# Router logits in four column groups, and token rows stored without their norm factor

## The chip, the cores and the metric

One NeuronCore of a Trainium2 chip runs the whole program. The metric is device time in microseconds (us) of one execution, lower is better. A run's time is a little longer than its span, which is the time from the first to the last instruction in the profile.

## The reference, cut to what matters

The program is one inference step of a two-layer encoder with D_MODEL = 1024, for 256 prompt frames and 64 sample frames (320 token rows, here called T). Layer 0 is a pooling mixer and a dense SwiGLU, then comes a shared K/V projection, and layer 1 is windowed attention followed by a top-2-of-8 mixture of experts. The change is in the mixture:

```
h = _rmsnorm(x, g_ffn)                     # x * rsqrt(mean(x*x) + eps) * g, per token row
logits = h @ w_router + b_router           # 1024 -> 8, in fp32
vals, idx = top_k(logits, 2); gates = softmax(vals)
y = sum over e of gate[:, e] * ((silu(h @ w1[e]) * (h @ w3[e])) @ w2[e])
```

A token goes to two experts only, so the kernel gathers the rows of each expert's tokens. The norm factor r of a token is a scalar per row: h = r * (x * g).

## The kernel before, in words

All activations are kept transposed (128 features x 320 tokens per chunk, eight chunks, KC = 8). Each fp32 weight unit of 1 MB (128 x 2048) is loaded into `raw` by SyncE's queue (6 slots), split by ScalarE (`hi`, L426: high part, two halves) and VectorE (`lo`, L1199: what is left, two halves) into a ring of 3, and multiplied by TensorE as three fp32r products (`mm3`, all matmuls at L720). The order of the work on each engine is written out by hand, and semaphores join the engines.

The stretch around the change lies between the attention's output projection and the first expert:

1. Output projection: four units, `dense` two column chunks each (f = 0, 1). VectorE adds each chunk into `xT` (L1466), ScalarE squares it (L438) and writes x * g to `hT` (L454, `weighted`, counted by `h_ready`), VectorE sums the squares (L1224).
2. TensorE: `rows(0)` transposes chunks 0 to 3 of `hT` back to token rows (L1037, 12 transposes into three PSUM banks); `logits` multiplies `hT` blocks of 128 or 64 tokens (as weights) by the 8 router columns (24 matmuls, each two instructions); `norm_columns` gives the sums of squares per token row; `rows(1)` transposes chunks 4 to 7.
3. ScalarE: root of the sums (L447, L448), the table load for Exp (L433), then six copies of the transposed rows to `hrow` (L655), each with the norm factor `rsc` as its scale, so that they wait for `rs_ready`; the gates' Exp (L659) stands among them.
4. SyncE's queue stores the rows to `rows_dram` in three transfers (L297), one per block of token rows, each when both halves of its block are copied.
5. VectorE: logits * rsc + bias (L1480), top two (L1484, L1487), selection `sel` (L1499). TensorE counts positions (`pos_done`); VectorE makes the one-hot matrices `Pm` (L1539), then the softmax gates (L1543 to L1548); TensorE multiplies `Pm` by the slot numbers; VectorE derives the gather index `ix` (L1550, L1552) after the gates. GpSimd splits the gates into three bf16 parts (`gpart`, L392 to L398) in four steps that start at `gate_ready`, and only then comes to its waits for `rows_stored` and `ix_ready` and to the indirect gather (L389).
6. TensorE fills its time with the embedding product of layer 1 (`embed`, eight chunks of six matmuls, whose banks are copied out by ScalarE at L530).
7. When the gathered rows land, TensorE transposes them (L1075), ScalarE and VectorE split them (L665, L1204), and the first expert starts.

The experts run in a loop: 8 turns here, 42 units each. In a turn ScalarE applies Silu to the gate product (L685, 7 times), VectorE multiplies by the up product (L1584), and the row results are scaled by the gate of their slot, `gs` (L707). SyncE's queue starts the loads of the loop once the first gather has landed.

Of the kernel before, what the change touches and what calls it, by code (L numbers as in the profile page):

```python
# [18 lines left out]
BF16 = mybir.dt.bfloat16  # L19
# [6 lines left out]
P = 128  # L26
# [40 lines left out]
EBANK = (4, 0, 5, 2, 6, 3, 4, 0)  # L67
LBANK = (7, 1, 7)
# [8 lines left out]
def build(nc, A):  # L77
    ctx = ExitStack()
    with ctx:
# [27 lines left out]
        wr = sb("wr", [P, KC, NE])  # L107
# [16 lines left out]
        tg = sb("tg", [P, 3, 5], BF16)  # L124
# [4 lines left out]
        sn, gs = sb("sn", [P, 2]), sb("gs", [P, 1])  # L129
# [35 lines left out]
        def squared(k):  # L165
# [49 lines left out]
        pT_done, pT_ready, pv_done, oh_ready, ol_ready = sem("pT_done"), sem("pT_ready"), sem("pv_done"), sem("oh_ready"), sem("ol_ready")  # L215
        lg_done, top_ready, gexp_ready, sel_ready, pos_done, routed = (sem(n) for n in (
            "lg_done", "top_ready", "gexp_ready", "sel_ready", "pos_done", "routed"))
        hrow_done, hrow_ready = sem("hrow_done"), sem("hrow_ready")
# [15 lines left out]
        def _(sp):  # L234
# [93 lines left out]
        def _(pool):  # L328
# [61 lines left out]

            pool.wait_ge(gate_ready, 1)
# [7 lines left out]
            pool.wait_ge(rows_stored, 48)  # L399
# [14 lines left out]
        def _(act):  # L414
# [236 lines left out]
            for n in range(6):  # L651
                t, half = n // 2, n % 2
                r = TS if t == 2 else P
                act.wait_ge(hrow_done, 4 + t if half else t + 1)
                nc.scalar.activation(hrow[0:r, t, 512 * half:512 * half + 512], PS[0:r, EBANK[n], :], ACT.Copy,  # L655
                                     scale=rsc[0:r, t:t + 1]).then_inc(hrow_ready, 1)
                if n == 3:
                    act.wait_ge(top_ready, 1)
                    nc.scalar.activation(rt[:, :, 1], rt[:, :, 0], ACT.Exp).then_inc(gexp_ready, 1)  # L659
# [15 lines left out]
            def turn(at, last):  # L675
# [5 lines left out]
                for n in range(NU):  # L681
                    kind, b = SEQ[n // 2]
                    if n % 2 and kind == "g":
                        act.wait_ge(unit_done, at(NU) + (Q_MOE + n + 1))
                        nc.scalar.activation(sgm[:, b % 2, :], PS[:, 2 + 2 * (b % 2), :], ACT.Silu).then_inc(msilu_done, 1)  # L685
# [7 lines left out]
                    if n == NU - 1:  # L693

                        act.wait_ge(gs_ready, at(1) + 1)
# [22 lines left out]
        def _(pe):  # L718
# [150 lines left out]
            def embed(layer, q, ns):  # L869
# [4 lines left out]
                for n in ns:  # L874
                    c = ORDS[layer][n]
                    bank = EBANK[n] if layer else c
                    if not layer:
                        pe.wait_ge(x_ready, KC + n + 1)
                    elif n < 6:
# [153 lines left out]
            def rows(half):  # L1033
                for t in range(3):
                    r = TS if t == 2 else P
                    for q in range(4):
                        last = nc.tensor.transpose(PS[0:r, EBANK[2 * t + half], P * q:P * q + P], hT[:, 4 * half + q, P * t:P * t + r], ident[:, :])  # L1037
                    last.then_inc(hrow_done, 1)

            def logits(k0, k1, blocks):  # L1040
                for k in range(k0, k1):
                    for t in blocks:
                        r = TS if t == 2 else P
                        last = mm(PS[0:r, LBANK[t], 8 + NE * t:8 + NE * t + NE], hT[:, k, P * t:P * t + r], wr[:, k, :], k == 0, k == KC - 1,
                                  skip_group_check=True)
                return last
# [7 lines left out]
            pe.wait_ge(h_ready, 4)  # L1054
            rows(0)
            pe.wait_ge(small_loaded, 48)
            pe.wait_ge(h_ready, 6)
            logits(0, 6, (0, 1))
            pe.wait_ge(h_ready, KC)
            logits(6, KC, (0, 1))  # L1060
            norm_columns(4)
            logits(0, KC, (2,)).then_inc(lg_done, 1)
            rows(1)
# [14 lines left out]
            def slot_info():  # L1078
                for t in range(3):
                    last = mm(PS[:, 1, 0:5], Pm[:, t, :], tg[:, t, :], t == 0, t == 2)  # L1080
                last.then_inc(slots_done, 1)

            embed(1, Q_EMB, range(1))
# [4 lines left out]
            embed(1, Q_EMB, range(1, 4))  # L1088
            pe.wait_ge(P_ready, 1)
            slot_info()  # L1090
            embed(1, Q_EMB, range(4, KC))
# [93 lines left out]
        def _(v):  # L1185
# [99 lines left out]
            norm(1)  # L1285
            v.wait_ge(pool_stored, 32)
# [191 lines left out]
            for t in range(3):  # L1478
                r = TS if t == 2 else P
                last = nc.vector.scalar_tensor_tensor(out=lg[0:r, t, :], in0=PS[0:r, LBANK[t], 8 + NE * t:8 + NE * t + NE], scalar=rsc[0:r, t:t + 1],  # L1480
# [39 lines left out]
            def take_slots(count):  # L1520
                v.wait_ge(slots_done, count)
                nc.vector.reduce_sum(sn[:, 0:1], PS[:, 1, 0:2], AX.X)
                nc.vector.reduce_sum(sn[:, 1:2], PS[:, 1, 2:5], AX.X).then_inc(sn_ready, 1)
# [10 lines left out]
            def use_gates(count):  # L1534
                nc.vector.tensor_copy(gs[:, :], sn[:, 1:2]).then_inc(gs_ready, 1)
# [4 lines left out]
            last.then_inc(number_ready, 1)  # L1540
            v.wait_ge(gexp_ready, 1)
# [7 lines left out]
            v.wait_ge(number_done, 1)  # L1549
            nc.vector.reduce_sum(sn[:, 0:1], PS[:, 1, 0:2], AX.X).then_inc(number_taken, 1)  # L1550
            v.wait_ge(number_taken, 1)
            nc.vector.tensor_scalar(ix[:, :], sn[:, 0:1], float(T), float(T - 1), ALU.add, ALU.min).then_inc(ix_ready, 1)  # L1552
# [9 lines left out]
            nc.vector.reduce_sum(sn[:, 1:2], PS[:, 1, 2:5], AX.X).then_inc(sn_ready, 1)  # L1562
# [165 lines left out]
```

## Time and profile before

| what | us |
|---|---|
| median of 3 runs | 1494.49 (1494.62, 1494.49, 1489.64) |
| the profiled execution's own time | 1490.69 |
| its span | 1488.9 |
| last output-projection matmul issued | 466.02 |
| last chunk of `hT` written | 467.89 |
| first expert matmul issued | 489.44 |
| one expert turn | about 118.7 |

The mean granted TensorE clock is 0.995 of full speed. Times in the rows are us from the start of the span. In a timeline a row is: start, duration, engine, line, operation, output <- inputs, partitions x elements, count; in brackets, the idle time before it and what ended it. Consecutive like instructions are merged into one row with a count (x12). PEld rows are weight loads that run beside the matmuls. An fp32 matmul (both operands fp32) appears as two instructions.

### The profile page before, as it was taken

What the parts mean: (1) busy time and instruction counts of PE and PEld (TensorE: products, weight loads), DVE (VectorE), ACT (ScalarE), POOL (GpSimd) and SP (SyncE); (2) the same over time, 40 slices, a digit from 0 to 9 for tenths busy, and PEclk for the clock granted to TensorE, in tenths of its full rate; (3) what the DMA queues carried; (4) which work ended last, traced back from release to release, by engine and by line L of the source; (5) the groups of instructions that cost most, each with busy time, mean ns of one, the idle gap of its engine ahead of it and who ended that gap; (6) DMA issues with size and microseconds to landing.
All of it is one profiled execution on the core that took longest, in us unless ns stands there. A gap on an engine that the chain in (4) does not pass through costs nothing.

```text
span 1488.9 us, 23197 instructions
## 1 busy us (share of the span) xinstructions
PE 1458.2 (98%) x8006; PEld 1283.3 (86%) x8006; DVE 1201.0 (81%) x1438; ACT 1015.3 (68%) x1291; POOL 34.9 (2%) x62
## 2 busy tenths in 40 slices
PE   6999999999999999999999999999999999999997
PEld 6999999999979788888888888888888888888787
DVE  6744545458775899999999999899999999999897
ACT  5433333356685777877877877787777787787776
POOL 2000000000000000000000000000000000000000
PEclk9999999999998999999999999999999999999999
DMA  9444434435502899999999999999999999999951
GB/s 351 174 142 166 144 142 147 164 123 191 191 30 93 320 380 391 364 398 389 359 394 383 357 403 380 371 390 375 379 388 375 387 371 383 390 359 401 377 199 36
DMA packets 65459, 437.59 MB, mean 294 GB/s; under 512 B 8595, under 2 KB 10259, under 8 KB 14336
## 3 DMA queue, kind: packets, MB, share of 16 engines
q1 hardware_dynamic: 62224, 426.77, 74.1%
q0 software_dynamic: 2768, 9.89, 2.6%
q8 instruction: 31, 0.51, 0.1%
q10 hardware_dynamic: 416, 0.26, 0.1%
q14 instruction: 20, 0.16, 0.0%
HBM read 428.12 MB, written 8.77 MB: 293 GB/s over the span
## 4 chain that ended last, share of the span: by engine, by line
PE 91%; DVE 5%; ACT 2%; DMA 1%; issue 1%; SPq 0%; DVEq 0%; POOLq 0%; ACTq 0%
PE PS L720 88%; PE PS L1116 2%; DVE s_Sl L1199 1%; DMA s_raw<-in_w_trunk 1%; DVE s_Al L1212 0%; PE PS L1075 0%; ACT s_Sh L426 0%; DMA s_G<-rows_dram,s_ix 0%; DVE s_xT L1278 0%; DVE s_st L1425 0%; DVE s_G L1367 0%; ACT s_hT L438 0%; DVE s_Al L1204 0%; DVE s_G L1440 0%; PE PS L1149 0%
## 5 line engine op out<-in xcount | busy, mean ns | idle before, releaser
L1199 DVE TENSOR_TENSOR s_Sl<-s_raw,s_Sh 128x1024 fp32r<-128x1024 f32 x798 | 938.9, 1220 | 130.1 <-ACT s_Sh L426 126.9
L426 ACT ACTIVATE s_Sh<-s_raw 128x1024 fp32r<-128x1024 f32 x798 | 799.8, 1052 | 220.1 <-PE PS L720 219.4
L720 PE MATMUL PS<-s_Sh,s_Ah 128*128 128x512 f32 x1344 | 529.5, 394 | 1.2 <-DVE s_Al L1204 1.2
L720 PE MATMUL PS<-s_Sh,s_Al 128*128 128x512 f32 x1344 | 523.8, 390 | 0.0
L720 PE MATMUL PS<-s_Sl,s_Ah 128*128 128x512 f32 x1344 | 523.2, 389 | 0.0
L720 PE MATMUL PS<-s_Ah,s_Sh 128*128 128x320 f32 x1008 | 314.2, 312 | 5.8 <-DVE s_Al L1212 2.4
L720 PE MATMUL PS<-s_Al,s_Sh 128*128 128x320 f32 x1008 | 311.8, 309 | 0.0
L720 PE MATMUL PS<-s_Ah,s_Sl 128*128 128x320 f32 x1008 | 311.8, 309 | 0.0
L720 PEld LDWEIGHTS PS<-s_Sh,s_Al 128*128 128x128 f32 x1344 | 252.3, 188 | 53.1
L720 PEld LDWEIGHTS PS<-s_Sh,s_Ah 128*128 128x128 f32 x1344 | 252.3, 188 | 52.1 <-issue 1.4
L720 PEld LDWEIGHTS PS<-s_Sl,s_Ah 128*128 128x128 f32 x1344 | 252.6, 188 | 50.6
L720 PEld LDWEIGHTS PS<-s_Ah,s_Sh 128*128 128x128 f32 x1008 | 189.5, 188 | 8.2 <-DVE s_Sl L1199 3.4
L720 PEld LDWEIGHTS PS<-s_Al,s_Sh 128*128 128x128 f32 x1008 | 189.7, 188 | 0.2
L720 PEld LDWEIGHTS PS<-s_Ah,s_Sl 128*128 128x128 f32 x1008 | 189.5, 188 | 0.0
L486 ACT ACTIVATE s_sq<-s_sq 128x640 f32<-128x640 f32 x14 | 10.3, 739 | 74.9 <-DVE s_sq L1300 63.5
L1204 DVE TENSOR_TENSOR s_Al<-PS,s_Ah 128x512 fp32r<-128x512 f32 (+1 forms) x88 | 55.2, 647 | 6.7 <-ACT s_Ah L665 2.7
L685 ACT ACTIVATE s_G<-PS 128x512 f32<-128x512 f32 x56 | 33.6, 599 | 36.9 <-PE PS L720 36.9
L490 ACT ACTIVATE s_Ah<-s_G 128x640 fp32r (+1 forms) x14 | 10.2, 738 | 51.3 <-PE PS L720 47.0
L1204 DVE TENSOR_TENSOR s_Al<-s_G,s_Ah 128x640 fp32r<-128x640 f32 x14 | 11.5, 825 | 41.6 <-ACT s_Ah L490 41.6
L1300 DVE TENSOR_TENSOR s_sq<-PS,s_rstd 128x640 f32<-128x640 f32 x14 | 11.5, 824 | 40.8 <-PE PS L720 40.8
L1584 DVE TENSOR_TENSOR s_G<-s_G,PS 128x512 f32<-128x512 f32 x56 | 38.1, 680 | 0.0
L1116 PEld LDWEIGHTS PS<-s_ident,s_G 128*128 128x128 f32 x224 | 27.8, 141 | 7.4 <-DVE s_G L1584 0.5
(206 smaller groups left out, 594.7 us busy)
## 6 DMA issues: line engine op xcount, KB each, us to landing
s_raw<-in_w_moe SPq DMA_DIRECT2D x336, 1024.0 KB, 5.9
s_raw<-in_w_trunk SPq DMA_DIRECT2D x63, 1024.0 KB, 4.8
y_dram<-s_G POOLq DMA_DIRECT2D x3, 512.0 KB, 4.0
s_xT<-in_xT SPq DMA_DIRECT2D x2, 640.0 KB, 15.2
s_G<-in_x_rows SPq DMA_DIRECT2D x2, 512.0 KB, 5.7
rows_dram<-s_G SPq DMA_DIRECT2D x2, 512.0 KB, 2.7
s_G<-y_dram SPq DMA_DIRECT2D x2, 512.0 KB, 7.4
out_y<-s_G SPq DMA_DIRECT2D x2, 512.0 KB, 3.0
```

Of the source, the lines that this page charges most:

```text
L426: nc.scalar.activation(Sh[:, q % NSPL, o:o + UNIT // 2], raw[:, q % NRAW, o:o + UNIT // 2], ACT.Copy).then_inc(hi_ready, 1)
L486: nc.scalar.activation(sg, gmt, ACT.Silu).then_inc(silu_done, 2)
L490: nc.scalar.activation(view(Ah, o, 2 * T), src, ACT.Copy).then_inc(gh_ready, 1)
L685: nc.scalar.activation(sgm[:, b % 2, :], PS[:, 2 + 2 * (b % 2), :], ACT.Silu).then_inc(msilu_done, 1)
L720: return nc.tensor.matmul(out, w, m, start=start, stop=stop, **kw)
L1116: done = nc.tensor.transpose(PS[:, 0, P * q:P * q + P], gum[:, b % 2, P * q:P * q + P], ident[:, :])
L1199: last = nc.vector.tensor_tensor(Sl[:, q % NSPL, o:o + UNIT // 2], raw[:, q % NRAW, o:o + UNIT // 2], Sh[:, q % NSPL, o:o + UNIT // 2].bit ...
L1204: return nc.vector.tensor_tensor(out, x, high.bitcast(F32), ALU.subtract).then_inc(done, 1)
L1300: nc.vector.tensor_tensor(gmt, PS[:, bank:bank + 2, 0:T], rstd2, ALU.mult).then_inc(gm_ready, 1)
L1584: nc.vector.tensor_tensor(gum[:, b % 2, :], sgm[:, b % 2, :], PS[:, 3 + 2 * (b % 2), :], ALU.mult).then_inc(gum_ready, 1)
```

## The change

- The router weights are padded from 8 to 32 columns. Chunk k's logits are one matmul with `wr` as weights (32 columns) and all 320 tokens of `hT` moving, written to partitions 32 * (k % 4) of PSUM bank 7; so eight matmuls in four column groups. ScalarE copies bank 7 to `std`, and three small matmuls with a `fold` matrix (a 128 x 8 sum of identity blocks) add the four groups and turn the result to token rows.
- Rows are stored without the norm factor: the copies (`row_copy`) no longer have a scale and don't wait for it. The first halves are transposed between the two chunks of the last projection unit and copied before the last chunk is added; the rows are stored in six half-row transfers.
- The norm factor is carried to each slot: GpSimd splits `rsc` in three bf16 parts (four new instructions), `slot_info` gets three more columns, and the slot's factor is the Silu's scale in every turn. The gate weight is multiplied by it once on VectorE (one new instruction).
- The index of the first gather is computed ahead of the softmax gates; `embed` chunks 0 and 1 are moved ahead of the wait for the selection, chunk 2 ahead of the numbers, chunks 3 to 7 ahead of `slot_info`.

```diff
-        wr = sb("wr", [P, KC, NE])
+        wr = sb("wr", [P, KC, LGROUP])
+        fold = sb("fold", [P, NE])
@@ SyncE
-            for t in range(3):
-                r = TS if t == 2 else P
-                sp.wait_ge(hrow_ready, 2 * t + 2)
-                sp.dma_start(rows_dram[P * t:P * t + r, :], hrow[0:r, t, :]).then_inc(rows_stored, 16)
+            for half in range(2):
+                for t in range(3):
+                    r, o = TS if t == 2 else P, 512 * half
+                    sp.wait_ge(hrow_ready, 3 * half + t + 1)
+                    sp.dma_start(rows_dram[P * t:P * t + r, o:o + 512], hrow[0:r, t, o:o + 512]).then_inc(rows_stored, 16)
@@ GpSimd
+            pool.wait_ge(rs_ready, 1)
+            pool.tensor_copy(tg[:, :, 5], rsc[:, :]).then_inc(rpart_ready, 1)
...
+            pool.tensor_tensor(tg[:, :, 7], rrest[:, :], tg[:, :, 6], ALU.subtract).then_inc(rpart_ready, 1)
             pool.wait_ge(gate_ready, 1)
...
-            pool.wait_ge(rows_stored, 48)
+            pool.wait_ge(rows_stored, 96)
@@ ScalarE
+            def row_copy(t, half):
+                r, o = TS if t == 2 else P, 512 * half
+                act.wait_ge(hrow_done, 3 * half + t + 1)
+                nc.scalar.activation(hrow[0:r, t, o:o + 512], PS[0:r, RBANK[t], :], ACT.Copy).then_inc(hrow_ready, 1)
...
+                    if c == 6:
+                        for t in range(3):
+                            row_copy(t, 0)
...
+            act.wait_ge(part_logits, 1)
+            nc.scalar.activation(std[:, :], PS[:, 7, 0:T], ACT.Copy).then_inc(part_moved, 1)
+            row_copy(0, 1)
             root_columns(4)
+            row_copy(1, 1)
+            row_copy(2, 1)
             table(ACT.Exp)
-            act.wait_ge(rs_ready, 1)
...
+            act.wait_ge(top_ready, 1)
+            nc.scalar.activation(rt[:, :, 1], rt[:, :, 0], ACT.Exp).then_inc(gexp_ready, 1)
...
+                        if b == 0:
+                            act.wait_ge(gs_ready, at(1) + 1)
-                        nc.scalar.activation(sgm[:, b % 2, :], PS[:, 2 + 2 * (b % 2), :], ACT.Silu).then_inc(msilu_done, 1)
+                        nc.scalar.activation(sgm[:, b % 2, :], PS[:, 2 + 2 * (b % 2), :], ACT.Silu, scale=gs[:, 1:2]).then_inc(msilu_done, 1)
@@ TensorE
+            def logits(k):
+                o = LGROUP * (k % 4)
+                return mm(PS[o:o + LGROUP, 7, 0:T], wr[:, k, :], hT[:, k, :], k < 4, k >= 4, skip_group_check=True)
+
+            def folded():
                 for t in range(3):
                     r = TS if t == 2 else P
+                    last = mm(PS[0:r, 7, NE * t:NE * t + NE], std[:, P * t:P * t + r], fold[:, :], True, True)
+                last.then_inc(lg_done, 1)
...
+                    if u == 3 and f == 0:
+                        pe.wait_ge(h_ready, 4)
+                        for c in range(4):
+                            row_blocks(c)
+            pe.wait_ge(hrow_ready, 3)
+            pe.wait_ge(h_ready, KC - 1)
+            for c in (4, 5, 6):
+                row_blocks(c)
             pe.wait_ge(small_loaded, 48)
+            for k in range(KC - 1):
+                logits(k)
             pe.wait_ge(h_ready, KC)
+            logits(KC - 1).then_inc(part_logits, 1)
+            row_blocks(7)
             norm_columns(4)
+            pe.wait_ge(fold_ready, 1)
+            pe.wait_ge(part_moved, 1)
+            folded()
+            embed(1, Q_EMB, range(2))
             pe.wait_ge(sel_ready, 1)
@@ VectorE
+            link(nc.vector.memset(rsc[:, :], 1.0))
+            v.wait_ge(consts, 4)
+            nc.vector.reduce_sum(fold[:, :], ident[:, :].rearrange("p (g e) -> p e g", g=4)[:, 0:NE, :], AX.X).then_inc(fold_ready, 1)
...
+            link(nc.vector.tensor_tensor(rt[:, :, 0], rt[:, :, 0], rsc[:, :], ALU.mult))
```

## Rows read from the trace of the kernel before

**Rows 1.** The page: busy time of each engine, and the chain's shares.
```profile
PE 1458.2 (98%) x8006; PEld 1283.3 (86%) x8006; DVE 1201.0 (81%) x1438; ACT 1015.3 (68%) x1291; POOL 34.9 (2%) x62
PE 91%; DVE 5%; ACT 2%; DMA 1%; issue 1%; SPq 0%; DVEq 0%; POOLq 0%; ACTq 0%
```
**Rows 2.** Stretch of the first turn: us; PE, PEld, DVE, ACT, POOL busy; PEclk, DMA.
```profile
489.50:608.30 118.80, 118.80 (x544) 98.52 (x545) 108.09 (x112) 91.58 (x100) 1.18 (x1) 1.00 0.98 373
```
**Rows 3.** The chain of waits, 455 to 492 us: start, duration, what.
```profile
477.93 1.14 ACT s_G L655 x2
479.09 2.86 DMA rows_dram<-s_G
...
482.87 4.21 DMA s_G<-rows_dram,s_ix
...
489.44 2.77 PE PS L720 x11
```
**Rows 4.** Timeline of VectorE and GpSimd, 473 to 482 us.
```profile
475.02 0.48 DVE L1480 SCALAR_TENSOR_TENSOR s_lg<-PS,s_rsc,s_br 128x8 f32<-128x8 f32 x3 [1.14 <-PE PS L720]
...
477.23 0.18 DVE L1499 TENSOR_TENSOR s_sel<-s_eq,s_valid 128x24 bf16<-128x24 f32 x1
...
479.94 0.18 DVE L1548 TENSOR_TENSOR s_gate<-s_gate,s_oh 128x24 f32<-128x24 f32 x1
...
481.10 0.24 POOL L398 TENSOR_TENSOR s_gpart<-s_grest,s_gpart 128x24 bf16<-128x24 f32 x1
```
**Rows 5.** Timeline of TensorE, 466 to 479 us.
```profile
466.17 1.47 PE L1037 MATMUL PS<-s_ident,s_hT 128*128 128x128 f32 x12
467.48 4.57 PE L720 MATMUL PS<-s_wr,s_hT 128*128 128x8 f32 x32
471.90 1.29 PE L720 MATMUL PS<-s_ones,s_sq 128*128 128x1 f32 x6
473.05 1.85 PE L720 MATMUL PS<-s_wr,s_hT 128*64 128x8 f32 x16
474.84 2.82 PE L1037 MATMUL PS<-s_ident,s_hT 128*128 128x128 f32 x12
...
478.69 0.47 PE L720 MATMUL PS<-s_Ah,s_Sh 128*128 128x320 f32 x1
478.95 0.47 PE L720 MATMUL PS<-s_Al,s_Sh 128*128 128x320 f32 x1
```
**Rows 6.** Timeline of TensorE: a 320-column fp32 product amid dense matmuls.
```profile
343.01 0.70 PE L720 MATMUL PS<-s_sq,s_ones 128*128 128x320 f32 x2
...
343.69 0.31 PE L720 MATMUL PS<-s_Al,s_Sh 128*128 128x320 f32 x1
```
**Rows 7.** Timeline of TensorE: attention products on parts of the array.
```profile
409.06 1.31 PE L720 MATMUL PS<-s_G 64*64 64x96 f32 x24
410.30 0.66 PE L1002 MATMUL PS<-s_ident,s_G 128*128 128x128 f32 x4
...
435.54 2.43 PE L720 MATMUL PS<-s_sq,s_G 128*64 128x128 f32 x40
437.91 0.42 PE L720 MATMUL PS<-s_Ah,s_Sh 128*128 128x320 f32 x1
```
**Rows 8.** Three stretches: busy times as in rows 2, granted clock third from the end.
```profile
441.00:466.00 25.00, 25.00 (x172) 25.00 (x171) 12.95 (x19) 13.14 (x22) 0.00 (x0) 1.00 0.36 127
...
470.00:471.00 1.00, 1.00 (x6) 1.00 (x7) 0.00 (x0) 0.00 (x0) 0.00 (x0) 0.50 0.00 0
...
481.00:482.00 1.00, 1.00 (x9) 1.00 (x8) 0.34 (x2) 1.00 (x2) 0.27 (x2) 1.00 0.32 70
```
**Rows 9.** Groups of instructions by shape, ScalarE: busy, mean ns, idle before.
```profile
L685 ACT ACTIVATE s_G<-PS 128x512 f32<-128x512 f32 x56 | 33.6, 599 | 36.9 <-PE PS L720 36.9
L707 ACT ACTIVATE s_G<-PS,s_gs 128x512 f32<-128x512 f32 x14 | 8.9, 687 | 5.5 <-PE PS L720 5.5
```
**Rows 10.** Timeline of ScalarE inside a turn of the loop.
```profile
630.62 2.01 ACT L426 ACTIVATE s_Sh<-s_raw 128x1024 fp32r<-128x1024 f32 x2 [0.71 <-PE PS L720]
```

More of the change, by code:

```diff
@@ L66 @@
 ORDS = ((4, 5, 6, 7, 0, 1, 2, 3), (0, 1, 2, 3, 4, 5, 6, 7))
-EBANK = (4, 0, 5, 2, 6, 3, 4, 0)
-LBANK = (7, 1, 7)
+EBANK = (0, 2, 3, 4, 5, 6, 0, 2)
+RBANK = (4, 5, 6)
+LGROUP = 32
 STATB = {1: 7, 2: 7, 3: 7, 4: 1, 5: 7, 6: 7}
@@ L123, in build @@
         posm = sb("posm", [P, 3, NE])
-        tg = sb("tg", [P, 3, 5], BF16)
+        tg = sb("tg", [P, 3, 8], BF16)
+        rrest = sb("rrest", [P, 3])
         gpart = sb("gpart", [P, 3, NE, 3], BF16)
@@ L128, in build @@
         PT = sb("PT", [P, T], F32R)
-        sn, gs = sb("sn", [P, 2]), sb("gs", [P, 1])
+        sn, gs = sb("sn", [P, 3]), sb("gs", [P, 2])
         ix, ixn, ixs = sb("ix", [P, 1], U32), sb("ixn", [P, 1], U32), sb("ixs", [P, 1], U32)
@@ L645, in _ @@
                     weighted(G_FFN1, 4, c, c + 1)
+                    if c == 6:
+                        for t in range(3):
+                            row_copy(t, 0)
                 if u < 2:
                     hi(Q_O + u + 4)
+            act.wait_ge(part_logits, 1)
+            nc.scalar.activation(std[:, :], PS[:, 7, 0:T], ACT.Copy).then_inc(part_moved, 1)
+            row_copy(0, 1)
             root_columns(4)
+            row_copy(1, 1)
+            row_copy(2, 1)
             table(ACT.Exp)
-            act.wait_ge(rs_ready, 1)
[L651 to L659, printed above, removed]
+            act.wait_ge(top_ready, 1)
+            nc.scalar.activation(rt[:, :, 1], rt[:, :, 0], ACT.Exp).then_inc(gexp_ready, 1)
             table(ACT.Silu)
@@ L693, in turn @@
                     if n == NU - 1:
-                        act.wait_ge(gs_ready, at(1) + 1)
                         if not last:
@@ L878, in embed @@
                         pe.wait_ge(x_ready, KC + n + 1)
+                    elif n < 3:
+                        pe.wait_ge(h_ready, KC)
                     elif n < 6:
@@ L1032, in _, with row_blocks @@
             outputs(KC - 1)
-            def rows(half):
+            def row_blocks(c):
+                for t in range(3):
+                    r, q = TS if t == 2 else P, c % 4
+                    last = nc.tensor.transpose(PS[0:r, RBANK[t], P * q:P * q + P], hT[:, c, P * t:P * t + r], ident[:, :])
+                    if q == 3:
+                        last.then_inc(hrow_done, 1)
+            def logits(k):
+                o = LGROUP * (k % 4)
+                return mm(PS[o:o + LGROUP, 7, 0:T], wr[:, k, :], hT[:, k, :], k < 4, k >= 4, skip_group_check=True)
+            def folded():
                 for t in range(3):
                     r = TS if t == 2 else P
[L1036 to L1046, printed above, removed]
+                    last = mm(PS[0:r, 7, NE * t:NE * t + NE], std[:, P * t:P * t + r], fold[:, :], True, True)
+                last.then_inc(lg_done, 1)
             for u in range(4):
@@ L1079, in slot_info @@
                 for t in range(3):
-                    last = mm(PS[:, 1, 0:5], Pm[:, t, :], tg[:, t, :], t == 0, t == 2)
+                    last = mm(PS[:, 1, 0:8], Pm[:, t, :], tg[:, t, :], t == 0, t == 2)
                 last.then_inc(slots_done, 1)
-            embed(1, Q_EMB, range(1))
+            embed(1, Q_EMB, range(2, 3))
             pe.wait_ge(number_ready, 1)
@@ L1087, in _ @@
             last.then_inc(number_done, 1)
-            embed(1, Q_EMB, range(1, 4))
+            embed(1, Q_EMB, range(3, KC))
+            pe.wait_ge(rpart_ready, 4)
             pe.wait_ge(P_ready, 1)
             slot_info()
-            embed(1, Q_EMB, range(4, KC))
             pe.wait_ge(eple_ready, KC + 8)
@@ L1479, in _ @@
                 r = TS if t == 2 else P
-                last = nc.vector.scalar_tensor_tensor(out=lg[0:r, t, :], in0=PS[0:r, LBANK[t], 8 + NE * t:8 + NE * t + NE], scalar=rsc[0:r, t:t + 1],
+                last = nc.vector.scalar_tensor_tensor(out=lg[0:r, t, :], in0=PS[0:r, 7, NE * t:NE * t + NE], scalar=rsc[0:r, t:t + 1],
                                                       in1=br[0:r, :], op0=ALU.mult, op1=ALU.add)
@@ L1534, in use_gates @@
             def use_gates(count):
-                nc.vector.tensor_copy(gs[:, :], sn[:, 1:2]).then_inc(gs_ready, 1)
+                nc.vector.tensor_copy(gs[:, :], sn[:, 1:3]).then_inc(gs_ready, 1)
             v.wait_ge(stepped, 1)
@@ L1540, in _ @@
             last.then_inc(number_ready, 1)
+            v.wait_ge(number_done, 1)
+            nc.vector.reduce_sum(sn[:, 0:1], PS[:, 1, 0:2], AX.X).then_inc(number_taken, 1)
+            v.wait_ge(number_taken, 1)
+            nc.vector.tensor_scalar(ix[:, :], sn[:, 0:1], float(T), float(T - 1), ALU.add, ALU.min).then_inc(ix_ready, 1)
             v.wait_ge(gexp_ready, 1)
```

24 lines of the change are left out of this document (10 added, 14 removed).

## The prediction

> **What bounds the kernel now.** I read the page's busy shares and the chain of waits first: TensorE is busy for 98% of the span and makes up 91% of the chain [rows 1]. So only TensorE's own work, or a place where it stands still, can move the time. The loop of experts takes eight turns of 118.7 us in which TensorE has no idle time (118.80 of 118.80 us [rows 2]), and the change removes nothing from them. What it touches is the stretch between the output projection and the first expert matmul, which was issued at 489.44. Next I read the chain through it [rows 3]: it ends with the last two row copies at 477.93 to 479.07, the store of the rows to DRAM (2.86 us), GpSimd's issue (0.92 from 481.95 to the transfer's start), the gather (4.21), and 2.4 us of transposes and splits. The whole stretch from the last projection matmul (start 466.2) is 23.3 us; that is 1.6% of the time, and a good part of it is latency that the change does not touch: 0.92 + 4.21 + 2.4 = 7.5 us behind the release of the gather, and the routing chain on VectorE. So the change has only some 16 us to work in, before anything is costed.
>
> The second thing to see is who else is nearly as late. GpSimd's last gate part ends at 481.34 [rows 4], and the rows are stored at 481.95 [rows 3]. GpSimd runs in order, and the gather stands behind the gate parts. So the edit that lets the rows go early can win only 481.95 - 481.34 = 0.6 us by itself; beyond that the gather waits for logits, selection, gates, gate parts. The gain has to come from an earlier start of that chain, which begins at 475.02 with the scaled logits [rows 4] behind TensorE's last logit matmul.
>
> **The change part by part, up to the logits.** The 12 transposes of the first half took 467.48 - 466.17 = 1.31 us [rows 5]. They move between the two chunks of the last projection unit, so the second chunk, its addition, square and weighting come 1.3 us later (the last chunk is weighted at 467.9 now, 469.2 then). Copies of the first halves run on ScalarE in the meantime: three copies from 466.1 at about 0.55 us (two scaled ones took 1.14 [rows 3]), done at 467.8. TensorE, finished with the projection at 467.5, waits some 0.3 us for them, since the next transposes go to the same banks. Nine transposes at 0.109: done at 468.8.
>
> The logits: before, 48 instructions in 4.42 (467.48 to 471.90) + 1.79 (473.05 to 474.84) = 6.2 us [rows 5]. After, eight fp32 products of 320 columns. The same shape is seen once per norm: between dense matmuls that follow each other every 0.147 us (25.00 us for 172 recorded ones, 0.145 [rows 8]), it starts at 343.01 and the second dense matmul behind it at 343.69, so it costs 343.69 - 0.147 - 343.01 = 0.53 us [rows 6]. In series that is 8 x 0.53 = 4.3 us. Whether the four column groups overlap no row shows for 32 columns. The nearest are the attention products [rows 7]: 12 score products on 64 x 64 parts, of 1536 columns together, would take 1536/320 x 0.53 = 2.5 us in series and took 1.24 (409.06 to 410.30): twice as fast. Two sets of ten output products (128 x 64 parts, 1024 columns each) took 437.91 - 435.54 = 2.37 us, against 3.4 in series: 1.4 times. Bounds: 4.3 us (no overlap) and 1.1 (all four). I take twice as fast, 2.1 us, and one half product more at the end, 2.4: each product is two instructions on the same group, and only the second of one and the first of the next can be side by side, which fits the scores.
>
> The Trainium skill (TensorE: Matmul & The Clock Gate, part on packing small matmuls) gives 2.38 times for three column groups; by that the eight would take about 1.8 us, an estimate, and the sum would be 0.6 us better. The Trainium skill (TensorEngine Tiling, Key Properties) also says that a change of tiling mode drains the array, which speaks against the change, since it goes from transposes to 32 columns and back twice. The trace has the nearest thing at 437.91: the first dense matmul after the 64-column products takes 0.42 instead of 0.31 us, so 0.1 us a switch, 0.4 at most in all.
>
> So the last logits end at about 471.2. Then three transposes (0.33), the norm columns (6 instructions; 1.15 us from 471.90 to 473.05, at half clock [rows 5, 8], 0.65 at full), meanwhile ScalarE copies the partial logits (128 x 320, under 0.55), one row copy (0.55) and takes the roots; three fold products (6 instructions, 0.65). Logits done at 472.9, the norm factor on VectorE at about the same time, against 475.02: 2.1 us earlier. The added copy and fold products are in this (about 1.1 us that were not there before).
>
> **From the logits to the gather.** VectorE's chain keeps its length to the one-hots. `embed` 0 and 1 now stand ahead of the selection: 12 matmuls, 1.8 us at 0.147 and about 3.2 at half clock, where the starts lie 0.26 to 0.27 apart (478.69, 478.95 [rows 5]). The selection comes 2.4 us after the logits' start, 475.4; TensorE gets there from 472.8 at 474.5 at full clock, or 476.0 at half: a new wait of 0.6 us for the positions. The softmax chain now stands behind the slot numbers (PE products, a reduction and the index: about 0.7 us) and has one more linked operation (0.2). GpSimd's four steps from `gate_ready` took 481.34 - 480.12 = 1.2 us [rows 4] and stay; its four new ones come right after the norm factor and are done 3 us before the gates. The table load for the Exp follows the last row copy at 473.8; with some 1.5 us for it the Exp can run at 475.3, before it is needed.
>
> At full clock: one-hots done at 477.05, index at 477.8, gates at 479.05, gate parts at 480.3. Rows are stored at 473.8 + 2.9 = 476.7 and bind no longer. The gather is released at 480.3 instead of 481.95: 1.7 us gained. With half clock from the fold products on: 0.6 for the positions and 0.2 for the chunk and the numbers are lost, 0.9 gained. TensorE's embedding is done by 482, before the rows land at 486; `slot_info` (three more columns, moved behind all of it) is at 481.6, and its user on VectorE has 3 us in hand. ScalarE copies embeddings until 482.
>
> The granted clock: it is 1.00, the 2.4 GHz level, up to about 470, 0.50, the 1.2 GHz level, from there, and 1.00 again by 481 [rows 8], after TensorE had run transposes and eight-column matmuls since 466.2. The new stretch has 320-column work in their place but also short waits. I take half clock from about the fold on, full clock before it.
>
> **The loop and the start.** Each Silu gets a scale from SBUF: 599 ns without, against 687 for a scaled copy of the same shape [rows 9], 0.09 us x 56 = 4.9 us of ScalarE. It is hidden: ScalarE's splits wait 0.71 us for TensorE at each unit [rows 10], and the split behind a Silu has a unit's time (2.72 us) of lead over its use. If that cover were gone it would cost up to 4.9 us. The new wait for `gs` at a turn's first Silu is for something written at the end of the turn before. The new DVE work near 45 us (0.4 us) lies under a unit of TensorE. SyncE's six stores queue before a wait that ends with the gather, and hold nothing back; the loop's loads start with the gather as before.
>
> Sum: -0.9 us, with 1.7 as the good end at two-fold overlap.
>
> **The time.** The profiled execution took 1490.69, so it would become 1489.8. The median shown is 3.8 us above it; the four executions (1489.64, 1490.69, 1494.49, 1494.62) scatter by 5 us with a mean of 1492.4. I put the forecast on that mean: 1491.5.
>
> **Rivals.** (1) The logits stage gives nothing: half clock starts at 470 as before. Then half the logits and all behind them take twice as long: logits done at 474.9, the selection waits for `embed` to 478.1, index before gates, gate parts at 483.0, gather 1.0 us later than now. With logits in series as well, about 2 us more: 1493 to 1496. For it: the fall of the clock at 470 in [rows 8]; against: the denser products. Chance 0.30. (2) The slower side beyond that: the scaled Silu delays the split behind it, TensorE waits for `lo` at each of 56 blocks, +4.9 - 0.9 = +4.0 us, 1496.4. It decides if the lead over TensorE is under 0.09 us; the 0.71 us idle before each split speaks against. Chance 0.05. (3) Better: four-fold overlap and full clock throughout. Logits end when the last chunk is weighted (469.2 + 0.3), 1.3 us earlier again: -3 us, 1489.4. Chance 0.13. (4) Something in the layout of the loop's code or of the transfers shifts the whole by more than this stretch could: 0.04. My forecast: 0.48.
>
> **Range and chances.** All but (4) lie within 5 us of the mean, and the executions themselves scatter by 2.5 to either side: 1487.0 to 1496.5. A change under 0.5% (7.5 us) can't be told from none here. No case but (4) reaches it, save with the scatter: faster 0.06, same 0.90, slower 0.04.
>
> **What would show it.** The first expert matmul at about 488.5; rows stored before 477; the wait before the gather ended by GpSimd's gate part; eight logit products within 2.4 us, against 4.3 or 1.1; PEclk between 468 and 473; Silu at about 0.69 us with no idle TensorE in the turns. Wrong would be a turn longer than 118.8 us, or a first expert matmul after 489.5.

## The result, and the profile after

Over 22 runs each, the changed kernel takes 1490.31 us (1488.83 to 1492.19), the kernel before 1492.62 us (1489.13 to 1494.62): a ratio of 0.9988 with a 95% interval of 0.9982 to 0.9993, so 2.3 us median to median, and 1.0 to 2.7 us by the interval. The forecast was 1491.5 in a range of 1487.0 to 1496.5, with the change within 0.5%.

First the chain of waits of the changed kernel, from the output projection to the first expert (start, duration, what); it answers to [rows 3].

```profile
461.37 1.31 PE PS L1059 x12
462.68 3.51 PE PS L741 x24
466.20 1.18 PE PS L1059 x9
467.38 1.21 PE PS L741 x16
...
474.64 0.24 PE PS L741 x3
...
477.44 0.07 POOL s_gpart L412
477.51 0.63 issue
...
478.36 4.43 DMA s_G<-rows_dram,s_ix
...
485.62 14.51 PE PS L741 x55
```

The reader is to see that the row store is gone from it and that a gate part on GpSimd (L412) stands before the gather's issue. L1059 x12 are the transposes that now lie between the two chunks of the last projection unit. L741 x16 are the logits: 1.21 us.

Then TensorE's timeline in two stretches, which answers to [rows 5].

```profile
467.31 1.28 PE L741 MATMUL PS<-s_hT,s_wr 128*32 128x320 f32 x16
468.52 0.55 PE L1059 MATMUL PS<-s_ident,s_hT 128*128 128x128 f32 x3
468.91 0.71 PE L741 MATMUL PS<-s_ones,s_sq 128*128 128x1 f32 x6
469.55 0.82 PE L741 MATMUL PS<-s_fold,s_std 128*128 128x8 f32 x6
...
479.23 0.23 PE L741 MATMUL PS<-s_tg,s_Pm 128*128 128x8 bf16 x3
482.93 1.94 PE L1109 MATMUL PS<-s_ident,s_G 128*128 128x128 f32 x8 [3.48 <-DMA s_G<-rows_dram,s_ix]
485.62 0.79 PE L741 MATMUL PS<-s_Sh,s_Ah 128*128 128x512 f32 x1 [0.75 <-DVE s_Al L1238]
486.21 0.63 PE L741 MATMUL PS<-s_Sl,s_Ah 128*128 128x512 f32 x1
486.63 0.63 PE L741 MATMUL PS<-s_Sh,s_Al 128*128 128x512 f32 x1
```

And stretches of it, with the columns of [rows 2] (granted clock third from the end), which answer to [rows 8].

```profile
470.00:471.00 1.00, 1.00 (x9) 0.96 (x9) 0.68 (x5) 1.00 (x3) 0.42 (x3) 1.00 0.56 213
...
478.00:479.00 1.00, 1.00 (x9) 1.00 (x8) 0.10 (x1) 0.54 (x2) 0.64 (x1) 1.00 0.00 0
...
482.00:484.00 2.00, 1.07 (x5) 1.10 (x6) 0.36 (x4) 0.00 (x0) 0.00 (x0) 0.63 0.04 16
484.00:486.00 2.00, 1.25 (x6) 0.85 (x5) 1.16 (x2) 1.69 (x3) 0.00 (x0) 0.50 0.34 66
486.00:488.00 2.00, 2.00 (x6) 1.52 (x6) 1.74 (x3) 1.39 (x2) 0.00 (x0) 0.50 1.00 422
```

The half clock that lay over the routing work from 470 to 480 is gone from there. It has come back later: TensorE stands idle for 3.48 us, because the embedding is done and the rows are not there, and from about 482.5 to 489.3 it is granted the 1.2 GHz level. The eight transposes take 1.94 us instead of 1.06, and the first expert matmuls are 0.42 us apart instead of 0.23. The same rows of the kernel before, at full clock:

```profile
487.21 1.06 PE L1075 MATMUL PS<-s_ident,s_G 128*128 128x128 f32 x8 [0.74 <-DMA s_G<-rows_dram,s_ix]
489.44 0.49 PE L720 MATMUL PS<-s_Sh,s_Ah 128*128 128x512 f32 x1 [1.17 <-DVE s_Al L1204]
489.77 0.40 PE L720 MATMUL PS<-s_Sl,s_Ah 128*128 128x512 f32 x1
490.00 0.39 PE L720 MATMUL PS<-s_Sh,s_Al 128*128 128x512 f32 x1
```

The two profiles can't be laid on each other by their own clocks. The changed kernel's starts earlier: its first pooled products are at 16.44 us, those of the kernel before at 17.83. So all that follows is measured from one mark in each trace, the chain piece that starts with the last attention products (435.61 before, 434.18 after). The table has this distance for three events, in us; "to turn 2" is the part from the first expert matmul to the same place in the second turn.

| kernel | gather transfer | first expert matmul | mark in turn 2 | to turn 2 |
|---|---|---|---|---|
| before | 47.26 | 53.83 | 163.17 | 109.34 |
| before, once more (e12) | 46.76 | 54.38 | 165.79 | 111.41 |
| changed | 44.18 | 51.44 | 162.54 | 111.10 |
| changed, once more (e8) | 44.18 | 50.91 | 163.06 | 112.15 |
| e1 TensorE kept at work | 44.18 | 50.96 | 160.29 | 109.33 |
| e2 gather first | 42.05 | 49.03 | 161.29 | 112.26 |
| e3 before, gather first | 45.44 | 56.00 | 165.36 | 109.36 |
| e4 index after the gates | 43.51 | 50.66 | 161.84 | 111.18 |
| e5 one column group | 47.40 | 54.49 | 165.42 | 110.93 |
| e6 two column groups | 45.27 | 51.87 | 162.53 | 110.66 |
| e7 Silu without scale | 44.19 | 51.40 | 162.17 | 110.77 |
| e9 gather and split first | 42.05 | 49.17 | 158.50 | 109.33 |
| e10 gather first, TensorE kept at work | 42.05 | 49.04 | 158.39 | 109.35 |
| e11 all three | 42.06 | 49.86 | 159.20 | 109.34 |

The change brings the gather forward by 3.1 us and the first expert by 2.4 us. The last column is 109.33 to 109.36 in every kernel whose first expert runs at full clock, and 110.7 to 112.3 in the others: 1.3 to 2.9 us are given back there. Behind that nothing differs: from the mark in turn 2 to the end of the span it is 890.1 to 890.7 us in all fourteen traces, and the next turn, from mark to mark, is 118.61 us in both first profiles. So two profiles differ only ahead of the first mark (the start) and between it and the mark in turn 2.

### The profile page after: what moved, and what is told of

Same layout as the page of the kernel before. It is cut to its first block, busy times and chain, and to the rows that moved or that the text cites. A ratio compares the mean times of both kernels' runs of the same rounds, so it can differ in the third digit from the quotient of the medians.

```text
span 1487.1 us, 23157 instructions
## 1 busy us (share of the span) xinstructions
PE 1454.6 (98%) x7980; PEld 1278.0 (86%) x7980; DVE 1199.4 (81%) x1441; ACT 1020.2 (69%) x1292; POOL 36.6 (2%) x66
## 4 chain that ended last, share of the span: by engine, by line
PE 91%; DVE 6%; ACT 1%; issue 1%; POOL 1%; DMA 0%; DVEq 0%; POOLq 0%; ACTq 0%
PE PS L741 88%; PE PS L1150 2%; DVE s_Sl L1233 1%; DVE s_Al L1246 0%; PE PS L1109 0%; DMA s_G<-rows_dram,s_ix 0%; ACT s_Sh L440 0%; DVE s_xT L1312 0%; DVE s_st L1462 0%; DVE s_G L1404 0%; DVE s_Al L1238 0%; DVE s_G L1477 0%; ACT s_hT L452 0%; PE PS L1059 0%; PE PS L1183 0%
## 5 line engine op out<-in xcount | busy, mean ns | idle before, releaser
L741 PE MATMUL PS<-s_Sh,s_Ah 128*128 128x512 f32 x1344 | 530.3, 395 | 0.8 <-DVE s_Al L1238 0.8
L741 PE MATMUL PS<-s_Sh,s_Al 128*128 128x512 f32 x1344 | 524.4, 390 | 0.0
L741 PE MATMUL PS<-s_Sl,s_Ah 128*128 128x512 f32 x1344 | 524.0, 390 | 0.0
L741 PE MATMUL PS<-s_Ah,s_Sh 128*128 128x320 f32 x1008 | 313.6, 311 | 5.4 <-DVE s_Al L1246 2.4
L741 PE MATMUL PS<-s_Ah,s_Sl 128*128 128x320 f32 x1008 | 311.5, 309 | 0.0
L741 PE MATMUL PS<-s_Al,s_Sh 128*128 128x320 f32 x1008 | 311.4, 309 | 0.0
L741 PEld LDWEIGHTS PS<-s_Sh,s_Al 128*128 128x128 f32 x1344 | 252.7, 188 | 53.3
L741 PEld LDWEIGHTS PS<-s_Sh,s_Ah 128*128 128x128 f32 x1344 | 252.8, 188 | 52.0 <-issue 1.1
L741 PEld LDWEIGHTS PS<-s_Sl,s_Ah 128*128 128x128 f32 x1344 | 253.0, 188 | 50.8
L741 PEld LDWEIGHTS PS<-s_Ah,s_Sh 128*128 128x128 f32 x1008 | 189.2, 188 | 7.8 <-issue 3.4
L741 PEld LDWEIGHTS PS<-s_Al,s_Sh 128*128 128x128 f32 x1008 | 189.3, 188 | 0.2
L741 PEld LDWEIGHTS PS<-s_Ah,s_Sl 128*128 128x128 f32 x1008 | 189.2, 188 | 0.0
L707 ACT ACTIVATE s_G<-PS,s_gs 128x512 f32<-128x512 f32 x56 | 38.6, 689 | 37.0 <-PE PS L741 37.0
```

Source lines behind the costliest of these rows:

```text
L741: return nc.tensor.matmul(out, w, m, start=start, stop=stop, **kw)
```

## The experiments

Edits are to the changed kernel unless it says before. A ratio is to the kernel before.

**e1: TensorE kept at work.**

```diff
                 last.then_inc(slots_done, 1)
...
+            for _ in range(6):
+                mm(PS[:, 7, 0:T], ones[:, :], hT[:, 0, :], True, True)
             pe.wait_ge(eple_ready, KC + 8)
```

> The changed kernel with six 320-column fp32 products into PSUM bank 7 behind slot_info, about 0.53 us each, 3.2 us in all, results unused; they fill TensorE's wait for the gathered rows (479.4 to 482.9). Theory A (the changed kernel gives back a part of its gain because TensorE idles 3.5 us and then runs at half clock until 489): granted clock 1.00 through the stretch, transposes of the gathered rows 1.1 us instead of 1.9, the first 8 expert matmuls 0.23 us apart instead of 0.43; 2.0 to 2.6 us faster than the changed kernel, some 4.5 faster than before. Rival B (the clock falls regardless, or the loop's load or the splits hold the start): no change within 0.3 us.

1488.26 us, ratio 0.9971 (0.9962 to 0.9981). TensorE's timeline:

```profile
482.21 3.48 PE L741 MATMUL PS<-s_hT,s_ones 128*128 128x320 f32 x12
485.72 1.06 PE L1109 MATMUL PS<-s_ident,s_G 128*128 128x128 f32 x8
488.04 0.50 PE L741 MATMUL PS<-s_Sh,s_Ah 128*128 128x512 f32 x1 [1.26 <-DVE s_Al L1240]
488.37 0.39 PE L741 MATMUL PS<-s_Sl,s_Ah 128*128 128x512 f32 x1
488.60 0.39 PE L741 MATMUL PS<-s_Sh,s_Al 128*128 128x512 f32 x1
```

Useless work at the same gather time (44.18) takes 2.25 us off the mark in turn 2, 0.48 at the first expert and 1.77 behind it: the transposes take 1.06 us and the expert matmuls are 0.23 apart. Theory A holds: the wait cost more than its own length.

**e2: the gather ahead of the gate parts.**

```diff
+            pool.wait_ge(rows_stored, 96)
+            pool.wait_ge(y_summed, 64)
+            gather_rows(1)
             pool.wait_ge(gate_ready, 1)
...
-            pool.wait_ge(rows_stored, 96)
-            pool.wait_ge(y_summed, 64)
-            gather_rows(1)
```

> The changed kernel with GpSimd's waits for rows and index and the gather itself ahead of the four gate parts. Theory A (the gate parts on GpSimd's queue hold the gather; rows at 472.8 and index at 475.25 are ready): gather transfer starts at about 476.2 instead of 478.4, rows land at 480.6, TensorE idles only about 1.2 us and keeps its clock: first expert matmul 2 us earlier and its first matmuls at full clock, 3.5 to 4.5 us faster than the changed kernel in all; VectorE's split of unit Q_O + 6 (until 482.05) may hold the splitting of the gathered rows by 0.5 us. Rival B (the gate parts come too late when they stand behind the gather, so slot_info and the gates' copy hold the start instead): 0 to 1 us gained.

1487.52 us, ratio 0.9968 (0.9956 to 0.9980). GpSimd, TensorE and VectorE in it:

```profile
478.33 1.04 POOL L395 DMA_INDIRECT s_G<-rows_dram,s_ix  x1 [4.78 <-DVE s_ix L1581]
```

```profile
482.70 1.06 PE L1109 MATMUL PS<-s_ident,s_G 128*128 128x128 f32 x8 [1.15 <-DMA s_G<-rows_dram,s_ix]
485.31 0.79 PE L741 MATMUL PS<-s_Sh,s_Ah 128*128 128x512 f32 x1 [1.55 <-DVE s_Al L1238]
485.90 0.63 PE L741 MATMUL PS<-s_Sl,s_Ah 128*128 128x512 f32 x1
```

```profile
481.78 2.36 DVE L1233 TENSOR_TENSOR s_Sl<-s_raw,s_Sh 128x1024 fp32r<-128x1024 f32 x2
...
484.39 1.28 DVE L1238 TENSOR_TENSOR s_Al<-PS,s_Ah 128x512 fp32r<-128x512 f32 x2
```

The gather now waits for the index, and starts 2.1 us earlier, as theory A said. Its second half failed in this execution: the clock fell all the same, at about 484.7, behind two idle times of 1.15 and 1.55 us. It cost 2.9 us behind the first expert. This was the slowest of the seven runs (1489.50; the fastest took 1484.73), and the others have no trace, so how often the clock falls in this kernel is not known. VectorE's split held the low parts by some 0.4 us (1.55 us of idle time, against 1.17 in e9).

**e3: the same move in the kernel before.** The edit is that of e2 with `rows_stored` 48.

> The kernel before with the same move of the gather ahead of the gate parts. Theory A (there the stored rows, at 481.95, end the wait, not the gate parts, which end at 481.34): no change, within 0.3 us. Rival B (the gate parts held the gather there too): 0.6 to 1.5 us faster.

1493.36 us, ratio 1.0014 (1.0004 to 1.0024): slower, and neither theory had it. TensorE:

```profile
482.86 0.24 PE L720 MATMUL PS<-s_tg,s_Pm 128*128 128x5 bf16 x3 [3.59 <-DVE s_tg L1558]
482.96 0.61 PE L720 MATMUL PS<-s_Ah,s_Sh 128*128 128x320 f32 x1
483.37 0.47 PE L720 MATMUL PS<-s_Al,s_Sh 128*128 128x320 f32 x1
```

There `slot_info` stands ahead of `embed` 4 to 7. With the gate parts behind the gather TensorE stands idle for 3.59 us before it, and the rest of the embedding runs behind it, at half clock, until after the rows have landed. In the changed kernel all of `embed` stands ahead of `slot_info`; that this order is what lets the gather go first without harm is argued from the two traces and was not tried by itself. On the gather itself theory A is borne out: its transfer starts 0.91 us behind the stored rows here (479.47 to 480.38) and 0.92 in the kernel before, so the gate parts had not held it. The 1.8 us by which it is earlier in the table are the rows', since the clock fell later in this execution.

**e4: the index after the gates.**

```diff
-            v.wait_ge(number_done, 1)
-            nc.vector.reduce_sum(sn[:, 0:1], PS[:, 1, 0:2], AX.X).then_inc(number_taken, 1)
...
             nc.vector.tensor_tensor(gate[:, :, :], gate[:, :, :], oh[:, :, :], ALU.add).then_inc(gate_ready, 1)
+            v.wait_ge(number_done, 1)
+            nc.vector.reduce_sum(sn[:, 0:1], PS[:, 1, 0:2], AX.X).then_inc(number_taken, 1)
...
```

> The changed kernel with the gather's index computed after the softmax gates, as the kernel before has it. Theory A (the gather waits for the gate parts, not for the index): the gates come 0.5 to 0.6 us earlier, the gather too, so the move of the index was a loss of that much; 0.5 us faster than the changed kernel or more, as TensorE's idle time shrinks to 2.9 us. Rival B (the index ends the wait): 0.5 to 1 us slower.

The gather started 0.67 us earlier (43.51), the first expert 0.8 us (0.25 against the second profile of the changed kernel). The time, 1490.14 us (0.9988, 0.9980 to 0.9997), can't be told from the changed kernel's. The trace is with theory A: this part of the change costs 0.7 us at the gather, as long as the gather stands behind the gate parts.

**e5 and e6: one and two column groups.**

```diff
-                o = LGROUP * (k % 4)
-                return mm(PS[o:o + LGROUP, 7, 0:T], wr[:, k, :], hT[:, k, :], k < 4, k >= 4, skip_group_check=True)
+                return mm(PS[0:LGROUP, 7, 0:T], wr[:, k, :], hT[:, k, :], k == 0, k == KC - 1, skip_group_check=True)
```

(e6: `k % 2`, `k < 2`, `k >= KC - 2`; in both the copy and the fold take only the partitions in use.)

> The changed kernel with all eight logit products in one column group of 32 (accumulated there, no partial sums in the other groups). Theory A (four groups overlap four-fold: the eight took 1.2 us where one such product costs 0.53): eight in series, 4.3 us, first expert matmul 3.0 us later. Rival B (products of 32 columns are quicker in themselves and the groups do nothing): 1.2 to 1.5 us again and no loss.

> The changed kernel with the logits in two column groups. Theory A (time is eight products over the number of groups): 2.1 to 2.4 us for the products, 1.0 us later than with four. Rival B (the instructions of one product can't overlap with more than one neighbour, as the prediction had it): the same with two as with four groups.

The logits in the timelines of e5 and of e6:

```profile
469.82 4.49 PE L741 MATMUL PS<-s_hT,s_wr 128*32 128x320 f32 x16
```

```profile
471.15 2.35 PE L741 MATMUL PS<-s_hT,s_wr 128*32 128x320 f32 x16
```

From the first product to the transposes behind them it is 4.42, 2.28 and 1.21 us with one, two and four groups. The first expert is 3.05 us later with one group than with four, and 0.43 with two (against the changed kernel; 0.96 against its second profile). e5 takes 1493.61 us, ratio 1.0012 (0.9999 to 1.0024): without the overlap no gain can be seen. e6: 1491.46 us, 0.9994 (0.9982 to 1.0005). Theory A in both. With one group the gather starts at 47.40, no earlier than in the kernel before (47.26), so the rest of the change together brings nothing there. No run takes back the unscaled row copies or the new order of `embed` by itself.

**e7: Silu without its scale.**

```diff
-                        nc.scalar.activation(sgm[:, b % 2, :], PS[:, 2 + 2 * (b % 2), :], ACT.Silu, scale=gs[:, 1:2]).then_inc(msilu_done, 1)
+                        nc.scalar.activation(sgm[:, b % 2, :], PS[:, 2 + 2 * (b % 2), :], ACT.Silu).then_inc(msilu_done, 1)
```

> The changed kernel with Silu without its scale (the norm factor is left out of the Silu's argument, so the experts compute something else). Theory A (0.09 us more of ScalarE per Silu is hidden under its 0.71 us of idle time): Silu 0.60 instead of 0.69 us, turns of 118.6 us as before, no change within 0.3 us. Rival B (the longer Silu delays the splits): up to 4.9 us faster.

The Silus by shape, of the changed kernel and of e7 (busy, mean ns, idle before):

```profile
L707 ACT ACTIVATE s_G<-PS,s_gs 128x512 f32<-128x512 f32 x56 | 38.6, 689 | 37.0 <-PE PS L741 37.0
```

```profile
L707 ACT ACTIVATE s_G<-PS 128x512 f32<-128x512 f32 x56 | 33.6, 600 | 36.9 <-PE PS L741 36.9
```

5.0 us less of ScalarE, and 1490.84 us (0.9989, 0.9976 to 1.0002): no gain. The idle time ahead of the Silus stays 37 us, and from the mark in turn 2 to the end of the span it is 890.4 us with the scale and 890.7 without, so the scale is hidden whole.

**e8 and e12: each kernel once more.**

> The changed kernel once more, for how much a profile of the same program differs. Theory A: the start until the first pooled products differs by up to 1.5 us between executions (17.83 us before, 16.44 in the changed kernel), which has nothing to do with the change; the distance from the last attention products to the first expert turn repeats within 0.3 us if the clock falls at the same place, and by up to 3 us if it doesn't. Rival B: the start repeats at 16.4 us, so it belongs to the change.

> The kernel before once more, for its profile. Theory A (in the kernel before the half clock falls within the logits, selection and embedding, and where it begins and ends differs between executions, so its stage differs by up to 3 us): the distance from the last attention products to the first expert matmul differs from 53.8 us by 1 to 3 us and the logit instructions from 6.2 us, while the clock at the first expert is 1.00. Rival B (the stage repeats): 53.8 us within 0.3, and the scatter of the times comes from elsewhere.

e8: 1490.45 us. The gather is at 44.18 as in the first profile; what differs is the loss behind the first expert, 2.8 instead of 1.8 us. Here the clock fell only at about 486.8, so the transposes still ran at full clock:

```profile
485.32 1.07 PE L1109 MATMUL PS<-s_ident,s_G 128*128 128x128 f32 x8 [3.42 <-DMA s_G<-rows_dram,s_ix]
```

The start differs by 2.5 us (mark at 436.64 and 434.18), more than theory A allowed, and within the one program, so the 1.4 us between the first two profiles need not be the change's. e12: 1492.54 us, ratio 1.0000 (0.9987 to 1.0014). Its first expert is at 54.4, 0.6 us later than in the first profile, less than theory A said, and theory A was wrong too in that the clock at the first expert would be 1.00. Stretches of e12, and its row of the transposes:

```profile
472.00:474.00 2.00, 2.00 (x14) 1.98 (x13) 0.00 (x0) 0.16 (x1) 0.00 (x0) 0.50 0.00 0
474.00:476.00 2.00, 2.00 (x18) 1.98 (x18) 0.58 (x5) 1.97 (x5) 0.00 (x0) 0.50 0.04 8
...
488.00:490.00 2.00, 1.49 (x8) 1.46 (x8) 0.00 (x0) 0.48 (x1) 0.00 (x0) 0.66 0.00 0
490.00:492.00 2.00, 1.25 (x4) 0.82 (x3) 1.43 (x3) 1.74 (x4) 0.00 (x0) 0.50 0.52 131
```

```profile
488.51 1.83 PE L1075 MATMUL PS<-s_ident,s_G 128*128 128x128 f32 x8 [2.08 <-DMA s_G<-rows_dram,s_ix]
```

In this execution the kernel before has both half clocks, the one over the logits and the one at the first expert. TensorE was idle for 2.08 us ahead of the transposes, not 0.74. The gather's transfer took 4.91 instead of 4.21 us (its part on GpSimd 1.74 instead of 1.06; it began 0.4 us after the start of VectorE's split here, 0.2 us before it in the first profile), and the embedding, at full clock again from 478.4 (480.2 in the first profile), was done 1.1 us sooner after the mark, the gather begun only 0.5. So the first profile of before showed it from its better side, and the change's 0.6 us at turn 2 by the two first profiles (163.17 to 162.54) becomes 2.7 by the two second ones (165.79 to 163.06).

**e9, e10, e11: versions built on these.** In e9 VectorE's `lo(Q_O + 6)` is moved ahead of its wait for the gate parts, on top of e2; e10 is e2 with two of e1's products behind `slot_info`; e11 has both, and two products more behind the transposes of the gathered rows.

```diff
+            lo(Q_O + 6)
             v.wait_ge(gpart_ready, 4)
...
-            lo(Q_O + 6)
             place_slots(1)
```

> The gather ahead of the gate parts, and VectorE's split of unit Q_O + 6 (2.3 us) ahead of its wait for the gate parts, where VectorE idles 1.5 us. In the run with the gather first alone the split ended at 484.1 and held the low parts of the gathered rows, whose high part was there at 483.95. Theory A (the split holds the first expert and TensorE's idle time still ends in half clock): first expert matmul 0.3 us earlier, half clock for 2.9 us of loss again: 0.3 us faster than with the gather first alone, or not to be told from it. Rival B (an idle time shorter by 0.3 us keeps the clock): 3 us faster.

> The gather ahead of the gate parts and two 320-column products (1.1 us, results unused) behind slot_info, nothing else. [...] Rival B (the idle time behind the transposes, 1.5 us, is enough for the fall): same loss of 2.9 us.

> Gather first, split of Q_O + 6 early, two 320-column products ahead of the gathered rows' transposes and two behind them (1.1 us each, results unused). Theory A: both idle times are filled, clock 1.00 throughout, first expert matmul 51.4 - 2.7 = 48.7 us behind the last attention products, second turn 158.0 us behind them (163.2 before, 162.5 in the changed kernel): 4.5 to 5.5 us faster than before, 1486.5 to 1487.5. Rival B (products behind the transposes delay the first expert by up to 0.5 us and the clock falls later in the turn): 2.5 us faster than before.

| | us | ratio to before |
|---|---|---|
| e9 | 1486.91 | 0.9971 (0.9961 to 0.9982) |
| e10 | 1485.06 (4 runs) | 0.9955 (0.9938 to 0.9973) |
| e11 | 1486.63 | 0.9971 (0.9961 to 0.9981) |

The first expert of e9, and of e10:

```profile
481.94 0.22 PE L741 MATMUL PS<-s_tg,s_Pm 128*128 128x8 bf16 x3 [1.23 <-DVE s_tg L1597]
482.45 1.06 PE L1109 MATMUL PS<-s_ident,s_G 128*128 128x128 f32 x8 [0.30 <-issue]
484.68 0.50 PE L741 MATMUL PS<-s_Sh,s_Ah 128*128 128x512 f32 x1 [1.17 <-DVE s_Al L1238]
```

```profile
480.92 1.32 PE L741 MATMUL PS<-s_hT,s_ones 128*128 128x320 f32 x4
482.32 1.06 PE L1109 MATMUL PS<-s_ident,s_G 128*128 128x128 f32 x8
484.83 0.49 PE L741 MATMUL PS<-s_Sh,s_Ah 128*128 128x512 f32 x1 [1.45 <-DVE s_Al L1240]
```

All three kept the clock in the profiled execution. In e9 nothing was won by the earlier split (49.17 against 49.03), and the reason stands in GpSimd's and VectorE's rows:

```profile
478.62 2.04 POOL L409 CAST s_gpart<-s_gate 128x24 bf16<-128x24 f32 x1
478.23 2.34 DVE L1233 TENSOR_TENSOR s_Sl<-s_raw,s_Sh 128x1024 fp32r<-128x1024 f32 x2
```

The first gate part took 2.04 us instead of 0.24 (e2): it started while VectorE was splitting and ended with the split. So the gate parts came late, and TensorE waited for `slot_info`. The idle times of 1.23, 0.30 and 1.17 us, in place of e2's 1.15 and 1.55, didn't bring the clock down in the profiled execution, which was its rival's case. Over all its runs e9 can't be told from e2 (0.9961 to 0.9982 against 0.9956 to 0.9980), so how often it keeps the clock is not known. In e10 two useless products did it, with the same first expert as e2. In e11 the products behind the transposes delayed the first expert by 0.8 us and brought nothing. The three intervals overlap with each other and with e2's, so which of them is best is open; each has a median 3.4 to 5.3 us below the changed kernel's.

## Why the prediction was right or wrong

**What bounds the stretch: right.** It held that the gather would be released by the gate parts and not by the rows, and that the stored rows would bind no longer; the chain shows both. The place of the gain, an earlier start of the logits' chain, is right too: e5 takes that part away and the gain with it.

**The logits' products: wrong in size.** The step said twice as fast as in series and half a product more, 2.4 us, from two attention products on parts of the array. They took 1.21 us. The ratios 4.42, 2.28 and 1.21 for one, two and four groups show that the time goes with the number of groups, 3.7 times faster with four; the reason given, that only neighbouring halves of two products can be side by side, is refuted. The series price of 0.53 us from one norm product was right (4.42 for eight). The transposes, copies and what stands between them came as said: the logits began at 467.31, where the step, shifted by the 1.43 us between the marks, had 467.3. The Trainium skill (TensorE: Matmul & The Clock Gate, part on packing small matmuls) puts three column groups at 2.38 times, and it was the better guide here. The Trainium skill (TensorEngine Tiling (Array Packing), Key Properties) says that a change of tiling mode drains the array; little of that is to be seen: 4.42 us for eight products in series leaves at most 0.2 us for it.

**The chain from there: right.** From the scaled logits to the gates the step had 6.1 us (472.9 to 479.05), and the trace has 5.9 (470.53 to 476.47). Measured from the mark, the gather's release came 1.4 us earlier than the full-clock line said (43.3 against 44.7); 1.2 of it is the error of the logits.

**The clock: wrong twice.** The forecast had half clock from the fold on, for 0.8 us; it was 1.00 from there to 482. That, with four-fold overlap, is rival 3, and at the gather it came true: 3.1 us earlier, where rival 3 said 3 (but 1490.31 us in the end, where it said 1489.4). But no case looked at what TensorE does once nothing of the embedding is left. The forecast noted that the embedding ends by 482 and the rows land at 486, and took it as slack. In the kernel before the embedding, slowed by the half clock, filled that wait (0.74 us idle); the change pulled the gather forward by 3.1 us, the embedding by more, and left 3.48 us. It paid for that with half clock at the first expert. e1 shows the price: 1.8 to 2.8 us at the mark in turn 2, 2 us in the median. One of the forecast's own signs of being wrong came true by it, a turn longer than 118.8 us: the first turn became 1.8 us longer than before, though not by the Silu, and the next was as before.

**The Silu's scale: right.** 0.09 us each, hidden; e7.

**The time.** -0.9 us forecast, -2.3 measured at the median, inside the range. Two errors stand behind this, with opposite signs: at the gather 1.4 to 2.2 us more than forecast (3.1 against 1.7 at full and 0.9 at half clock), and 1.8 to 2.8 us given back. That they nearly cancel, so that the time came out close, is luck. By the first profile of the kernel before and the two of the changed one, 0.1 to 0.6 us of gain are left at the mark in turn 2 (163.17 against 163.06 and 162.54); the rest of the 2.3 is probably that the kernel before loses at the same place in some executions (e12), which its first profile didn't show. That is argued, not shown: how often it does can't be told from two profiles. The mean clock of whole executions doesn't tell either: e2's profiled one, with half clock at the first expert, has 0.997, and e1's, without it, 0.996. To put the forecast on the mean of the four executions and not on the median of three was right: over 22 runs the kernel before stands at 1492.62, where that mean was 1492.4.

## What to carry to other kernels

A wait on the engine that bounds the kernel has a price beyond its length if the engine's clock depends on its work: look at the first instructions after the wait, and if they are slower, move real work into it, or put in useless work as a test. Before an engine's small tasks are put in order, ask which of them starts a long transfer: on GpSimd the gather belonged ahead of the gate parts, worth 2.1 us, but only where nothing else queued behind those parts (e3). Lay traces on a common mark close to the change, and profile both kernels more than once when the effect is smaller than what an execution can differ by.

## What the runs showed of the hardware

- Fp32 products with 32-column weights and 320 moving columns in four column groups took 0.15 us each (1.21 for eight), 0.29 in two groups, 0.55 in one.
- TensorE fell to 0.50 of its clock after 3.48 us of idle time (changed kernel), after 1.15 + 1.55 us with 1.06 us of transposes between (e2), but not after 1.23 + 0.30 + 1.17 (e9) or after 1.26 alone (e1). Each of these is one execution. Idle time alone doesn't set it: in the kernel before it fell at 470 while the engine issued transposes and eight-column products without a gap, and in one execution (e3) only after 472. The Trainium skill (TensorE: Matmul & The Clock Gate, Why this matters for your kernels) warns of idle gaps between bursts of matmuls; the 3.48 us of the changed kernel agree, while e2 lost the clock behind shorter gaps and the kernel before, at 470, without one.
- A 128x24 cast on GpSimd took 2.04 us where it started during VectorE's split (e9; e11 the same), and 0.24 where VectorE was idle (e2, e10).
- The start of the same program, up to the mark, differed by 2.5 us between two executions (434.18 and 436.64), and the expert turn from the first matmul to the mark in turn 2 by 0.03 us in six traces at full clock.
